# Mixer gates and output products in row form: activations stationary, 512 weight columns moving

## The reference, cut to what matters

```python
def hybrid_mixer(u, ...):                       # u: (1, 256, 1024)
    xa, ya, q, k, v, g, sb, sc, sh, gates = jnp.split(u @ w_in, cuts, axis=-1)
    ha = rg_lru(causal_depthwise_conv(xa, lru_conv_w) + lru_conv_b, ...)   # recurrence over tokens
    oa = (ha * jax.nn.gelu(ya)) @ w_lru_out
    ret = retention(q, k, v, positions)         # 4 heads, each row of a head divided by its rms
    ob = (jax.nn.silu(g) * ret) @ w_ret_out     # w_ret_out: 2048 x 1024
    oc = (sb * causal_depthwise_conv(sc * sh, sc_conv_w)) @ w_sc_out
    ga, gb, gc = jnp.split(jax.nn.sigmoid(gates), 3, axis=-1)
    return (ga * oa + gb * ob + gc * oc) @ w_out
```

## Time and profile before

| | |
|---|---|
| Median of 3 runs | 2053.8 us (2053.3 to 2054.64) |
| The profiled execution, its own time | 2051.93 us |
| Its span, first to last instruction | 2050.1 us |
| TensorE matmuls busy | 2013.6 us, 98% |
| VectorE (DVE), ScalarE (ACT), GpSimd (POOL) busy | 64%, 47%, 5% |
| Mean granted TensorE clock | 0.998 |

### The profile page before, as it was taken

One profiled execution on the slowest core, in us unless ns is written; L12 is line 12 of the kernel. 1 busy time (PEld: TensorE's weight loads), 2 busy tenths in 40 slices (PEclk: granted clock), 3 DMA queues, 4 the chain that ended last, 5 costly groups with the idle time before them and its releaser, 6 DMA issues.

```text
span 2050.1 us, 31408 instructions
## 1 busy us (share of the span) xinstructions
PE 2013.6 (98%) x13308; PEld 1836.2 (90%) x13308; DVE 1318.6 (64%) x1617; ACT 971.1 (47%) x1334; POOL 102.9 (5%) x211
## 2 busy tenths in 40 slices
PE   9999999999999999999999999999999999999996
PEld 8888998999999888888889999999988888989985
DVE  7747767467556764766569755565667556766555
ACT  5445464434333543544455643443444445754343
POOL 1012000000000000100200000000010101010000
PEclk9999999999999999999999999999999999999999
DMA  7565455535556555565655564455655755355561
GB/s 261 191 205 195 144 186 191 179 124 180 190 185 206 163 186 193 177 204 186 195 185 165 165 206 144 159 181 180 201 187 168 237 188 177 128 159 185 185 205 63
DMA packets 282026, 369.53 MB, mean 180 GB/s; under 512 B 6679, under 2 KB 253751, under 8 KB 281886
## 3 DMA queue, kind: packets, MB, share of 16 engines
q1 hardware_dynamic: 276864, 352.34, 52.5%
q0 software_dynamic: 4528, 14.85, 2.3%
q10 hardware_dynamic: 494, 0.32, 0.1%
HBM read 366.28 MB, written 1.08 MB: 179 GB/s over the span
## 4 chain that ended last, share of the span: by engine, by line
PE 91%; DVE 4%; ACT 2%; issue 1%; POOL 1%; DMA 0%; DVEq 0%; POOLq 0%; ACTq 0%
PE ps L1496 19%; PE ps L1479 15%; PE ps L1467 13%; PE ps L1469 13%; PE ps L1468 13%; PE ps L1480 7%; PE ps L1557 4%; PE ps L1521 1%; DVE w_lo L975 1%; DVE u L1025 1%; PE ps L1630 1%; DVE a L1130 1%; ACT u L668 1%; PE ps L1815 1%; ACT a L662 0%
## 5 line engine op out<-in xcount | busy, mean ns | idle before, releaser
L975 DVE TENSOR_TENSOR w_lo<-raw,w_hi 128x1024 fp32r<-128x1024 f32 (+1 forms) x658 | 765.9, 1207 | 323.2 <-ACT w_hi L637 322.2
L637 ACT ACTIVATE w_hi<-raw 128x1024 fp32r<-128x1024 f32 (+1 forms) x658 | 653.0, 1041 | 394.0 <-PE ps L1496 205.2
L1467 PE MATMUL ps<-u,w_hi 128*128 128x256 f32 x1712 | 491.5, 287 | 1.7 <-DVE w_lo L975 1.6
L1469 PE MATMUL ps<-u,w_lo 128*128 128x256 f32 x1712 | 484.4, 283 | 0.0
L1468 PE MATMUL ps<-u,w_hi 128*128 128x256 f32 x1712 | 484.3, 283 | 0.0
L1479 PE MATMUL ps<-u,w_hi 128*128 128x512 f32 x1280 | 452.0, 398 | 0.0
L1480 PE MATMUL ps<-u,w_lo 128*128 128x256 f32 x1280 | 359.3, 281 | 0.0
L1467 PEld LDWEIGHTS ps<-u,w_hi 128*128 128x128 f32 x1712 | 328.4, 192 | 5.2 <-issue 4.7
L1468 PEld LDWEIGHTS ps<-u,w_hi 128*128 128x128 f32 x1712 | 328.4, 192 | 2.4 <-issue 1.9
L1469 PEld LDWEIGHTS ps<-u,w_lo 128*128 128x128 f32 x1712 | 328.4, 192 | 0.0
L1479 PEld LDWEIGHTS ps<-u,w_hi 128*128 128x128 f32 x1280 | 240.4, 188 | 59.3 <-issue 0.8
(11 more groups left out here) (273 smaller groups left out, 2341.0 us busy)
## 6 DMA issues: line engine op xcount, KB each, us to landing
raw<-in_w_mix_in_dram SPq DMA_DIRECT2D x112, 1024.0 KB, 5.1
raw<-in_ffn_w_in_dram SPq DMA_DIRECT2D x88, 1024.0 KB, 5.1
raw<-in_ffn_w_out_dram SPq DMA_DIRECT2D x40, 1024.0 KB, 5.0
raw<-in_w_ret_out_dram SPq DMA_DIRECT2D x16, 1024.0 KB, 5.2
raw<-in_w_up_dram SPq DMA_DIRECT2D x16, 1024.0 KB, 5.5
raw<-in_w_down_dram SPq DMA_DIRECT2D x16, 1024.0 KB, 5.0
raw<-in_w_in_dram SPq DMA_DIRECT2D x9, 1024.0 KB, 6.4
raw<-in_w_lru_out_dram SPq DMA_DIRECT2D x8, 1024.0 KB, 5.1
```

What stands on the lines that cost most here:

```text
L637: A(parts(n)[0][:, part], raw[i % RAW][:, part], ACT.Copy).then_inc(heads_done, 1)
L975: V.tensor_tensor(parts(n)[1][:, part], raw[i % RAW][:, part], parts(n)[0][:, part], ALU.subtract)\
L1467: M(dst[a], hi[:, k, c], act_hi[:, k0 + k, :], start=first and k == 0, stop=False)
L1469: ins = M(dst[a], lo[:, k, c], act_hi[:, k0 + k, :], start=False, stop=last and k == KD - 1)
```

## The change

Seven stages, `ga`, `lru_out`, `g`, `gb`, `ret_out`, `gc` and `sc_out`, 36 of the 76 slots of a mixer, go from the column form to a row form, `half_slot`: 4 k x 2 token tiles x 3 products = 24 matmuls of 512 columns. A slot now holds 512 columns by 4 k (rows of 2 KB in HBM, where it was 256 columns by 8 k, rows of 1 KB); two slots (four for `ret_out`) make one half of the result's columns, in two banks, one for each token tile (`half_bank`). The results are taken out of PSUM once for these two slots, in two instructions of 128x512, where it was one in each slot.

The head is now multiplied by its scale and by silu(g) in one DVE instruction for each token tile, before it is turned. `turn_head` stands a slot later, writes banks 7 and 4, and ACT copies its result to `h_hi`, DVE subtracting after it. The mixed sum, which is in row form now, has to be turned too: `turn_mixed`, 8 transposes after the third slot of `sc_out` and 8 after the first of `mix_out`, with ACT's copies (`mix_heads`) and DVE's subtractions (`mix_rests`) a slot later, in front of that slot's weight split.

```diff
+ROW_FORM = {"ga": 2, "lru_out": 2, "g": 2, "gb": 2, "ret_out": 4, "gc": 2, "sc_out": 2}
...
+        def half_bank(e, tt):
+            return ps[:, (2 + 2 * e) % 4 + tt, :]
+        def columns_of(a, e, tt):
+            return by_token(a)[:, tt, 512 * e:512 * e + 512]
+        def ret_bank(i):
+            return ps[:, 4 if i else 7, :]
...
+                        k, c = k0 + 4 * (j % per), c0 + 512 * (j // per)
+                        src = w[:, k:k + 4, c:c + 512]
...
+            def mix_heads(l, e):
+                for tt in range(TT):
+                    act.wait_ge(mix_turned.sem, mix_turned.at(l, 2 * e + tt + 1))
+                    A(u_hi[:, 4 * e:4 * e + 4, P * tt:P * tt + P], half_bank(e, tt).rearrange("p (k n) -> p k n", n=P),
+                      ACT.Copy).then_inc(mix_head.sem, 1)
...
+                        if name in ("g", "sc") and (m - 35) % 2 == 0 and 0 <= (m - 35) // 2 < HEADS:
+                            h = (m - 35) // 2
+                            act.wait_ge(ret_turned.sem, ret_turned.at(l, h + 1))
+                            for i in range(2):
+                                A(h_hi[:, 4 * h + 2 * i:4 * h + 2 * i + 2, :], ret_bank(i).rearrange("p (k n) -> p k n", n=S),
+                                  ACT.Copy).then_inc(ret_head.sem, 1)
+                        if (name, j) in (("sc_out", 3), ("mix_out", 1)):
+                            mix_heads(l, 0 if name == "sc_out" else 1)
...
-                        elif name == "gb":
-                            A(tiles(a4)[:, pair, :], pv, ACT.Sigmoid).then_inc(gb_ready.sem, 1)
+                        elif name == "gb" and j % 2 == 1:
+                            for tt in range(TT):
+                                A(columns_of(a4, j // 2, tt), half_bank(j // 2, tt), ACT.Sigmoid).then_inc(gb_ready.sem, 1)
...
-                            dve.wait_ge(ret_turned.sem, ret_turned.at(l, h + 1))
+                            dve.wait_ge(ret_scale.sem, ret_scale.at(l, h + 1))
                             dve.wait_ge(g_ready.sem, g_ready.at(l, 2 * h + 2))
-                            sg = a2[:, D * (h % 2):D * (h % 2) + D]
-                            own.done(V.tensor_tensor(sg, ps[:, 6:8, :].rearrange("p a n -> p (a n)"), sg, ALU.mult))
-                            split(sg.rearrange("p (k n) -> p k n", n=S), h_hi[:, 4 * h:4 * h + 4, :],
-                                  h_lo[:, 4 * h:4 * h + 4, :], ret_ready.sem)
...
+                            for tt in range(TT):
+                                ins = V.scalar_tensor_tensor(mul2[:, tt, :], ps[:, 5 + tt, :], ret_rs[:, tt:tt + 1],
+                                                             columns_of(a2, h % 2, tt), ALU.mult, ALU.mult)
+                            ins.then_inc(ret_scaled.sem, 1)
+                        if name in ("g", "sc") and (m - 35) % 2 == 0 and 0 <= (m - 35) // 2 < HEADS:
...
+                                dve.wait_ge(ret_head.sem, ret_head.at(l, 2 * h + i + 1))
...
+                                ins = V.tensor_tensor(h_lo[:, ks, :], ret_bank(i).rearrange("p (k n) -> p k n", n=S),
+                                                      h_hi[:, ks, :], ALU.subtract)
...
-                        elif name == "sc_out":
+                        elif name == "sc_out" and j % 2 == 1:
+                            e = j // 2
                             dve.wait_ge(slot_used, n + 1)
...
-                            own.done(V.tensor_tensor(tmp, pv, tiles(a4)[:, pair, :], ALU.mult))
-                            own.done(V.tensor_tensor(tmp, tmp, tiles(a5)[:, pair, :], ALU.add))
-                            split(tmp, u_hi[:, pair, :], u_lo[:, pair, :], mix_ready.sem)
...
+                            for tt in range(TT):
+                                acc = columns_of(a5, e, tt)
+                                own.done(V.tensor_tensor(mul2[:, tt, :], half_bank(e, tt), columns_of(a4, e, tt), ALU.mult))
+                                V.tensor_tensor(acc, acc, mul2[:, tt, :], ALU.add).then_inc(mixed.sem, 1)
...
             def turn_head(l, h):
                 pe.wait_ge(ret_scaled.sem, ret_scaled.at(l, h + 1))
+                if h < HEADS - 1:
+                    pe.wait_ge(ret_probs.sem, ret_probs.at(l, h + 2))
...
+            def half_slot(n, k0, act_hi, act_lo, e, first, last):
+                hi, lo = half_view(n)
+                for i in range(4):
+                    if i % 2 == 0:
+                        split_part(n, i // 2)
+                    for tt in range(TT):
+                        tok = slice(P * tt, P * tt + P)
+                        for a, (stat, mov) in enumerate(((act_hi, hi), (act_hi, lo), (act_lo, hi))):
+                            ins = M(half_bank(e, tt), stat[:, k0 + i, tok], mov[:, i, :], start=first and i == 0 and a == 0,
+                                    stop=last and i == 3 and a == 2)
+                ins.then_inc(slot_used, 1)
+            def turn_mixed(l, e):
+                for tt in range(TT):
+                    pe.wait_ge(mixed.sem, mixed.at(l, 2 * e + tt + 1))
+                    for i in range(4):
+                        ins = nc.tensor.transpose(half_bank(e, tt)[:, P * i:P * i + P],
+                                                  columns_of(a5, e, tt)[:, P * i:P * i + P], ident[:, :])
+                    ins.then_inc(mix_turned.sem, 1)
...
                                 row_slot(n, (2 * j, 2 * j + 1), u_hi, u_lo, j == 0, False)
+                                if j == 0:
+                                    turn_mixed(l, 1)
...
+                        elif name in ROW_FORM:
+                            row_form(l, name, j)
+                            if name == "sc_out" and j == 2:
+                                turn_mixed(l, 0)
...
-                        if name == "g" and j % 2 == 1:
-                            turn_head(l, j // 2)
+                        if name in ("g", "sc") and (m - 34) % 2 == 0 and 0 <= (m - 34) // 2 < HEADS:
+                            turn_head(l, (m - 34) // 2)
```

More of the change, by code:

```diff
@@ new lines, in turn_mixed, with row_form @@
+            def turn_mixed(l, e):
+                for tt in range(TT):
+                    pe.wait_ge(mixed.sem, mixed.at(l, 2 * e + tt + 1))
[3 more added lines that the diff above has]
+                    ins.then_inc(mix_turned.sem, 1)
+            def row_form(l, name, j):
+                n = l * SLOTS + AT[name] + j
+                per = ROW_FORM[name]
+                e = j // per % 2
+                if j % per == 0:
+                    if name == "g" and j >= 4:
+                        pe.wait_ge(g_ready.sem, g_ready.at(l, j - 2))
+                    else:
+                        before = EMPTIED[BEFORE[name]]
+                        pe.wait_ge(before.sem, before.at(l, 2 * e + 2))
+                if name == "lru_out" and j == 0:
+                    pe.wait_ge(oa_ready.sem, oa_ready.at(l, 4))
+                if name == "ret_out" and j == 0:
+                    pe.wait_ge(ret_ready.sem, ret_ready.at(l, HEADS))
+                if name == "sc_out" and j == 0:
+                    pe.wait_ge(oc_ready.sem, oc_ready.at(l, 4))
+                ah, al = (h_hi, h_lo) if name in ("lru_out", "ret_out", "sc_out") else (u_hi, u_lo)
+                half_slot(n, 4 * (j % per), ah, al, e, j % per == 0, j % per == per - 1)
@@ L1725, in mixer @@
-                        ah, al = u_hi, u_lo
-                        if name == "lru_out":
-                            ah, al = h_hi, h_lo
-                            pe.wait_ge(oa_ready.sem, oa_ready.at(l, 4))
-                        if name == "sc_out":
-                            ah, al = h_hi, h_lo
-                            pe.wait_ge(oc_ready.sem, oc_ready.at(l, 4))
-                        column_slot(n, bank((2 + j) % 4), ah, al)
-                        if name == "xa" and j == 2:
-                            turn_back(3 * l + 1, (2, 3))
@@ L1735, in mixer @@
-                        if name == "g" and j % 2 == 1:
-                            turn_head(l, j // 2)
+                                last_rows(n, 4, u_hi, u_lo, rows_done.sem,
+                                          ready=[(mix_ready.sem, mix_ready.at(l, 3 + tt)) for tt in range(TT)])
+                        elif name in ROW_FORM:
+                            row_form(l, name, j)
+                            if name == "sc_out" and j == 2:
+                                turn_mixed(l, 0)
+                        else:
+                            if name == "sc":
+                                pe.wait_ge(g_ready.sem, g_ready.at(l, j + 5))
+                            elif name != "xa":
+                                before = EMPTIED[BEFORE[name]]
+                                pe.wait_ge(before.sem, before.at(l, j + 1))
+                            column_slot(n, bank((2 + j) % 4), u_hi, u_lo)
+                            if name == "xa" and j == 2:
+                                turn_back(3 * l + 1, (2, 3))
```

128 lines of the change are left out of this document (59 added, 69 removed).

## The result

The changed kernel takes 2033.78 us in the median of 4 runs (2033.15 to 2034.39), the kernel before on the same chip 2053.55 (4 runs, 2050.51 to 2054.64): a ratio of 0.9909, 95% interval 0.9897 to 0.9921. The forecast was 2035.2 us, with a range of 2031.5 to 2039.5. The profiled execution took 2034.39 us.

A forecast was written before the change was run, and what follows sets the result against it. TensorE was taken as the bound, its matmuls busy for 98% of the span. Two mixers at -11.05 + 1.74 us each give -18.6 us, from 2053.8 to 2035.2 us; range 2031.5 to 2039.5.

The forecast's parts named there:

- The pitch: In `half_slot`: matmuls 0.227 us apart, so a slot takes 5.45 us instead of 5.76.
- Rival D: In `half_slot`: the row form gains nothing, 240 ns a matmul, only the transposes' +3.5 us remain: 2057.3 us; 3%.
- `g`: The eight slots of `g` in each mixer: 0.31 us saved a slot, -2.5 us.
- Rival E: More than forecast: cheaper switch from attention's operand type, or `ga`'s wait shrinks, at most 3.7 us: 2031.5 us; 5%.
- `ga`: Four slots of `ga`: the second still waits for DVE's split, so 23.03 us, -1.0 a mixer.
- The mixed turns: `turn_mixed` twice a mixer, eight transposes each at 0.87 us: +1.74 us a mixer.
- The hand-offs at nothing: Before head turns, `attend`, mixed turns and `mix_out`: slots cover the other engines' work, so no added TensorE wait.
- Rival B: At some of 12 head and mixed hand-offs ACT or DVE is late: 2037.5 to 2045 us; 9%.
- Rival C: Slower: the chain at the head and mixed hand-offs is wholly uncovered, 40 us less 18.6: 2075 us; 2%.
- the head's cover: At `turn_head`: ACT's copies, squares and split end at 7.2 us, the slot at 9.3; split due a slot later.
- Loads: Weight loads come every 5.45 us instead of 5.76, landing 5.1 us after issue: no cost.
- The base: Whole kernel before: profiled execution of 2051.93 us, plus 1.9 us to the runs' median, 2053.8 us.

The follow-up runs named there:

- experiment 1: The changed kernel with each 512-column matmul of `half_slot` made as two of 256 columns; 2056.22 us.
- experiment 8: The changed kernel with the three products ordered hi-hi, lo-hi, hi-lo, so the stationary operand changes at every matmul; 2034.63 us.
- experiment 4: The changed kernel with DVE's split of `ga`'s second slot moved ahead of the recurrence's last step; 2033.75 us.
- experiment 7: The kernel of experiment 4 with ACT's and DVE's copies of `v0`'s result also moved behind the next slot split; 2031.96 us.
- experiment 2: The changed kernel with every transpose of `turn_mixed` made twice; 2038.17 us.
- experiment 3: The changed kernel with each `turn_mixed` a slot earlier, right behind its half, without the covering slot; 2045.34 us.
- experiment 6: The changed kernel with six more 128x512 copies on ACT ahead of its two copies of each turned head; 2034.79 us.
- experiment 5: The kernel before with only `g` in row form and the head work changed, all other stages left in column form; 2048.33 us.

## Why the prediction was right, step by step

- **The pitch.** Forecast 5.45 us a slot. The 12 slots of `gb` and `ret_out` took 65.31 us, 5.44 each, `lru_out` 21.77. Shown to be the number of instructions (a matmul with its load) by experiment 1, and not the sharing of an operand by experiment 8. The term of 24 instructions x 13 ns was right, though the row that was taken for its pattern was misread: `last_rows` doesn't change the operand at each matmul. Rival D is out.
- **`g`**, -2.5 forecast, -2.24 measured: 61.90 us and the 0.79 of the last head turn, which now stands behind the first slot of `sc`, against 64.93 with that turn. The term was 0.3 too large. A slot behind `scores` takes 5.56 us where 5.83 stood, one behind `attend` 5.86 to 5.90 for 6.15: 0.27 us saved and not 0.31, since the first matmuls of a slot in row form stand 0.230 to 0.236 us apart behind float32 work, and 0.227 elsewhere. Rival E, a cheaper change of type, had nothing to gain: what the forecast took for a price of the change isn't one (last section).
- **`ga`**, 23.03 forecast, 23.09 measured. Right in mechanism: the wait grew (from 0.93 to 1.16 us beyond the pitch, 1.1 forecast), because the second slot hung on DVE and not on the first. Experiments 4 and 7 show DVE's recurrence to be its cause, with ACT's copy of `v` as the next in line, which the forecast hadn't named.
- **The mixed turns**, +1.74 a mixer. Measured by experiment 2: 1.75.
- **The hand-offs at nothing.** No idle time stands before the head turns, `attend`, the mixed turns or `mix_out`. Experiment 3 uncovers the mixed hand-off and finds 3.0 us of work under a cover of 5.44; experiment 6 loads the head's with 3.7 us and it still doesn't show. Rivals B and C fell for the reason that was given; the head's cover is wider than the 2.1 us of the forecast's sum.
- **Loads.** 5.1 us to landing, as before, at 193 to 231 GB/s in the windows of `ga`, `v1`, `lru_out` and `gb` with `ret_out`. Nothing, as forecast.
- **The base.** 2 x 9.10 = 18.2 us of 18.6 forecast. That the time came out 1.4 us under the forecast and not 0.4 over it fits a base that was too high, which is argued and not shown: the forecast carried the 1.9 us between the profiled execution of before and a median of three, and 27 later runs of that kernel have medians of 2052.7 and 2052.19. From these, 18.2 us less is 2034.5 and 2034.0. So that the median lies this near the forecast is partly luck; the mixers, 9.10 us of 9.31, are not.

## What to carry to other kernels

Where TensorE is never idle, count its instructions: the same columns in matmuls of 512 instead of 256 gave 13 ns for each matmul saved, its load included, 0.3 us of a 5.76 us slot, and the turns that the other form needs took back a sixth of it. A chain through other engines cost nothing here as long as a whole slot lay between its ends (3.0 us under 5.44); put the next link one slot later rather than shorten it. When a wait is cleared from one queue, look for the same producer in the other queues before you time it.

## What the runs showed of the hardware, unexpected

**Two paces of one instruction sequence.** The feed-forward slots of 32 matmuls (512 and 256 columns in turn) take 5.55 us each from start to start or 5.65, with the same program, at a granted clock of 1.00 in both. Windows of the changed kernel over ten such slots in the second and in the third feed-forward:

```profile
694.99:750.45 55.46, 55.46 (x322) 48.90 (x321) 39.12 (x46) 27.53 (x35) 0.00 (x0) 1.00 0.59 190
883.45:939.99 56.54, 56.54 (x322) 49.05 (x321) 39.15 (x46) 27.53 (x35) 0.00 (x0) 1.00 0.57 187
```

There are four feed-forwards, two to a layer. Each begins with a run of 13 slots (the last with one of 7), and such a run takes on one pace in its second or third slot and keeps it to its end. The quick pace was held by the first feed-forward in the profile of before, by the second in the changed kernel's and in experiment 1's, by the third in those of experiments 3, 5, 6, 7 and 8, and by none in those of 2 and 4; the 7 slots of the last held it in the changed kernel alone. It is worth 1.4 us in a run of 13 slots and 0.7 in one of 7, and that is most of what stood outside the mixers in the result: +1.66 (0.4 of it a longer first slot), -1.34 and -0.77. So it can hide effects under some 2 us when single executions or medians of four are compared, and for the profiled one of experiment 4 it did. What decides it stays open: no run here was made to tell.

**Hardly a price for the change of type.** A float32 matmul of the program stands in the trace as two records (x2 in its row). TensorE's timeline in the changed kernel, the end of `attend` (float32) and the start of `half_slot`:

```profile
405.71 1.02 PE L1713 MATMUL ps<-a,probs 128*128 128x512 f32 x2
406.17 0.79 PE L1741 MATMUL ps<-w_hi,u 128*128 128x512 f32 x1
406.80 0.40 PE L1741 MATMUL ps<-w_lo,u 128*128 128x512 f32 x1
```

`attend`'s records start 0.43 us apart, the last at 406.14; `half_slot`'s first is recorded 0.03 later and its second at 406.80. The 0.66 us between are 0.43 for `attend`'s last and 0.23 for `half_slot`'s first: the sum of the two pitches. In the kernel before it is 0.03 + 0.52 against 0.43 + 0.12. The 0.39 us that the forecast read off a slot behind `attend` is the last float32 record's own time, booked in the slot's window, and neither form can save it. What is left of a price is small and new with the row form: its next few matmuls stand 0.230 to 0.236 us apart and not 0.227, about 0.05 us a slot.
